# Two sums of squares of a decoder kernel folded by VectorE before TensorE sums them, and the order of its start rewritten

## The chip, the cores and the metric

The kernel runs on one core of a Trainium2 chip. The metric is the device time of one execution in microseconds. Beside it one execution was profiled; all rows below are of that one.

## The reference, cut to what matters

Two layers (DEPTH = 2) over 256 tokens of 1024 features. Each layer: RMSNorm of x, one wide projection that feeds three mixers (a gated linear recurrence, a retention, a windowed attention), gates, an output projection; a cross-attention into 256 memory tokens; a product-key mixture of 16384 single-neuron experts, the largest part. A last RMSNorm. What the change touches:

```python
def rmsnorm(x, g):
    y = x * rsqrt(mean(x * x, axis=-1) + EPS)      # over the 1024 features
    return y * g
for l in range(DEPTH):
    h = rmsnorm(x, ln_mix[l])                      # sum of x's squares, once a layer here
    ... = split(h @ w_in[l])                       # first column tiles: rq, rk, rv, rg, ...
    x = x + mixers(...)
    x = x + cross(rmsnorm(x, ln_xq[l]), rmsnorm(mem, ln_xkv[l]), ...)   # mem's squares: the same for both layers
    x = x + peer_ffn(rmsnorm(x, ln_ffn[l]), ...)
```

## The kernel before, in words

Activations lie transposed: 128 partitions by 8 chunks (KC) of 256 tokens. All weights come as a stream of 128x1024 float32 tiles (512 KB) through `ring`, four slots; a group is four tiles, and tile g.s is slot s of group g. Each tile is split into `w_hi` (rounded, by ScalarE, `high_part`, L1003) and `w_lo` (ring minus w_hi, by GpSimd, `low_part`, L445, or in some places by VectorE, `low_whole`, L1543). TensorE multiplies hi by hi, hi by lo and lo by hi (`product3`, L514 to L516); a tile of 24 products takes it 2.88 us. A slot goes round: SyncE reloads the ring slot when the low part has been made, ScalarE may write the high part when TensorE has used the slot, the low part follows, then TensorE. Each engine's program is one list in a fixed order, with waits on semaphores; an engine that waits holds up all that stands behind.

The head of a layer. Tiles 0.0 and 0.1 are multiplied by x times the gain, without the norm (`first_chunks`), then 0.2, then the sum of squares, then 0.3, then group 1 (1.0 to 1.3) with results scaled by `rinv` afterwards, then group 2 with the normed x. ScalarE squares x in four pairs of chunks (L1020); VectorE folds them to two chunks (`fold_pair`, L1575); TensorE sums those over the partitions by two products with a matrix of ones (`folded_pairs`, L485, into bank 0). ScalarE takes the root (`take_root`, L1048) after it has cast tile 0.3 and loaded the table for Sqrt; VectorE inverts it (L1585) and scales the results (`first_evac`, L1638), which frees the banks for group 1; it also makes the low part of 0.3 just ahead of the inversion (L1543). Behind the root stand ScalarE's casts of 1.0 and 1.1, whose low parts are GpSimd's first two tiles of the layer. Between folds and low part VectorE has two copies of 4 columns (L1613, L1614), in the first layer also one of 128 columns (L1581).

The start of the program. SyncE loads half tiles of 0.0 and 0.1 (front), a small table, three constants, then 0.2 and 0.3; ScalarE issues the loads of `lbp` and of x in four pieces. Both engines split the halves as they come. TensorE runs 14 products of zeros first.

The memory's squares (first layer alone). ScalarE squares the 8 chunks of mem after group HQ (L1179); after group HI TensorE sums them by eight products with ones (`rms_sums`, L477, into bank 6), ScalarE takes the root (`minv`, L1198), and the window attention goes on in the same bank. Its results' next copies out are `evac` (L1089).

## Time and profile before

| | us |
|---|---|
| runs | 2377.94, 2378.47, 2379.53 (median 2378.47) |
| the profiled execution | 2379.11 |
| its span on the core | 2377.3 |
| TensorE busy | 2360.4 (99%) |
| VectorE, ScalarE, GpSimd busy | 1595.9 (67%), 1318.1 (55%), 1068.4 (45%) |
| share of TensorE in the chain that ended last | 98% |

The chain is followed back from the last instruction; TensorE's granted clock reads 1.00 in each stretch. In rows of the timelines the first number is the start, the second the duration, both in us; brackets hold the idle time before and what ended it.

### The profile page before, as it was taken

What the parts mean: (1) busy time and instruction counts of PE and PEld (TensorE: products, weight loads), DVE (VectorE), ACT (ScalarE), POOL (GpSimd) and SP (SyncE); (2) the same over time, 40 slices, a digit from 0 to 9 for tenths busy, and PEclk for the clock granted to TensorE, in tenths of its full rate; (3) what the DMA queues carried; (4) which work ended last, traced back from release to release, by engine and by line L of the source; (5) the groups of instructions that cost most, each with busy time, mean ns of one, the idle gap of its engine ahead of it and who ended that gap; (6) DMA issues with size and microseconds to landing.
All of it is one profiled execution on the core that took longest, in us unless ns stands there. A gap on an engine that the chain in (4) does not pass through costs nothing.

```text
span 2377.3 us, 44376 instructions
## 1 busy us (share of the span) xinstructions
PE 2360.4 (99%) x16162; PEld 2152.6 (91%) x16162; DVE 1595.9 (67%) x3266; ACT 1318.1 (55%) x2054; POOL 1068.4 (45%) x445
## 2 busy tenths in 40 slices
PE   8999999999999999999999999999999999999999
PEld 7999889999999888888889998899999998888887
DVE  7465624879995656777674656168799945667776
ACT  5676555565555555554465665555555555555544
POOL 5757877787773000000067578777877720000000
PEclk9999999999999999999999999999999999999999
DMA  7544554456677667777664445545566776677774
GB/s 246 170 150 150 179 176 161 160 179 220 242 242 260 203 210 224 247 246 237 213 210 158 162 158 187 171 157 166 180 230 239 245 243 204 219 231 233 243 247 168
DMA packets 186851, 485.36 MB, mean 204 GB/s; under 512 B 14304, under 2 KB 81120, under 8 KB 182112
## 3 DMA queue, kind: packets, MB, share of 16 engines
q1 hardware_dynamic: 179376, 442.20, 56.5%
q10 hardware_dynamic: 7344, 41.36, 5.0%
q8 instruction: 88, 1.44, 0.2%
q14 instruction: 43, 0.35, 0.1%
HBM read 448.91 MB, written 34.60 MB: 203 GB/s over the span
## 4 chain that ended last, share of the span: by engine, by line
PE 98%; DVE 1%; ACT 0%; DMA 0%; POOL 0%; issue 0%; ACTq 0%; DVEq 0%
PE banks L949 29%; PE banks L514 15%; PE banks L516 15%; PE banks L515 15%; PE banks L891 5%; PE banks L550 5%; PE banks L925 3%; PE banks L892 3%; PE banks L551 2%; PE banks L854 1%; PE banks L838 1%; PE banks L819 1%; PE banks L744 0%; DMA x<-in_x 0%; PE banks L477 0%; DVE o_r L1919 0%
## 5 line engine op out<-in xcount | busy, mean ns | idle before, releaser
L445 POOL TENSOR_TENSOR w_lo<-ring,w_hi 128x1024 fp32r<-128x1024 f32 x441 | 1068.2, 2434 | 853.5 <-ACT w_hi L1003 850.5
L1003 ACT ACTIVATE w_hi<-ring 128x1024 fp32r<-128x1024 f32 x774 | 816.7, 1056 | 416.2 <-PE banks L949 339.3
L514 PE MATMUL banks<-h_r,w_hi 128*128 128x256 f32 x2464 | 701.4, 285 | 0.5 <-DVE h_r L1611 0.4
L516 PE MATMUL banks<-h_r,w_lo 128*128 128x256 f32 x2464 | 696.6, 283 | 0.0
L515 PE MATMUL banks<-h_r,w_hi 128*128 128x256 f32 x2464 | 696.4, 283 | 0.0
L949 PE MATMUL banks<-w_hi,o_r 128*128 128x512 f32 x2048 | 560.5, 390 | 0.0
L514 PEld LDWEIGHTS banks<-h_r,w_hi 128*128 128x128 f32 x2464 | 471.4, 191 | 3.4 <-issue 1.6
L515 PEld LDWEIGHTS banks<-h_r,w_hi 128*128 128x128 f32 x2464 | 471.6, 191 | 0.6 <-issue 0.5
L516 PEld LDWEIGHTS banks<-h_r,w_lo 128*128 128x128 f32 x2464 | 471.6, 191 | 0.0
L949 PEld LDWEIGHTS banks<-w_hi,o_r 128*128 128x128 f32 x2048 | 380.0, 188 | 79.3
L2093 DVE TENSOR_TENSOR w_lo<-ring,w_hi 128x1024 fp32r<-128x1024 f32 x320 | 389.6, 1218 | 31.4 <-ACT w_hi L1003 31.4
L949 PE MATMUL banks<-w_lo,o_r 128*128 128x512 f32 x1024 | 317.4, 391 | 0.0
L949 PEld LDWEIGHTS banks<-w_lo,o_r 128*128 128x128 f32 x1024 | 192.2, 188 | 42.1
L2074 DVE SCALAR_TENSOR_TENSOR arena_r<-iota_f,arena,banks 128x256 fp32r<-128x256 f32 x512 | 211.0, 473 | 0.0
L1357 ACT ACTIVATE arena<-banks 128x256 f32<-128x256 f32 (+1 forms) x192 | 73.9, 385 | 247.2 <-PE banks L516 247.0
L2125 DVE TENSOR_TENSOR o_r<-arena,o_r 128x256 fp32r<-128x256 f32 x256 | 108.4, 423 | 139.0 <-ACT o_r L1411 139.0
L891 PE MATMUL banks<-h_r,w_hi 128*128 128x512 f32 x512 | 182.8, 397 | 0.0
L892 PE MATMUL banks<-h_r,w_lo 128*128 128x256 f32 x512 | 143.6, 280 | 0.0
L1089 ACT ACTIVATE arena<-banks 128x256 f32<-128x256 f32 x116 | 44.5, 384 | 159.0 <-PE banks L516 158.9
L2119 DVE TENSOR_TENSOR arena<-arena,o_f 128x256 f32<-128x256 f32 x256 | 107.9, 421 | 18.0 <-DMA o_f<-gates_dram 4.2
L2139 DVE TENSOR_TENSOR banks<-banks,arena 128x256 f32<-128x256 f32 x64 | 27.7, 432 | 135.3 <-PE banks L949 135.3
L891 PEld LDWEIGHTS banks<-h_r,w_hi 128*128 128x128 f32 x512 | 96.2, 188 | 22.9
(332 smaller groups left out, 3123.4 us busy)
## 6 DMA issues: line engine op xcount, KB each, us to landing
ring<-in_stream SPq DMA_DIRECT2D x774, 512.0 KB, 3.4
gates_dram<-o_f ACTq DMA_DIRECT2D x32, 1024.0 KB, 5.5
o_f<-gates_dram SPq DMA_DIRECT2D x32, 1024.0 KB, 7.0
arena<-in_mem ACTq DMA_DIRECT2D x2, 1024.0 KB, 8.3
arena<-in_keys ACTq DMA_DIRECT2D x2, 1024.0 KB, 6.5
arena<-in_c_decay ACTq DMA_DIRECT2D x2, 768.0 KB, 4.8
ring<-in_stream SPq DMA_DIRECT2D x4, 256.0 KB, 6.0
x<-in_x ACTq DMA_DIRECT2D x4, 256.0 KB, 7.6
```

The lines of the kernel that those rows point to most:

```text
L445: pool.tensor_tensor(w_lo[:, s, :], ring[:, s, :], w_hi[:, s, :], ALU.subtract).then_inc(sem(f"low{s}"), 1)
L514: pe.matmul(out, lhs[0], rhs[0], start=first, stop=False)
L515: pe.matmul(out, lhs[0], rhs[1], start=False, stop=False)
L516: return pe.matmul(out, lhs[1], rhs[0], start=False, stop=last)
L550: pe.matmul(wide_out(s), hi, src[:, :, k, :], start=(k == 0), stop=False)
L891: pe.matmul(wide_out(parity), hi, h_r[:, :, k, :], start=(k == 0), stop=False)
L892: m = pe.matmul(tile_out(parity), lo, hr[0][:, k, :], start=False, stop=(k == KC - 1))
L949: m = pe.matmul(bank[:, 2 * t + half, :], gated_r[v][:, parity, t * P:(t + 1) * P], (w_hi, w_lo)[u][:, s, half * 512:(half + 1) * 512], st ...
L1003: act.activation(w_hi[:, s, :], ring[:, s, :], ACT.Copy).then_inc(sem(f"high{s}"), 1)
L2074: ins = dve.scalar_tensor_tensor(one2[:, parity, t], bc(iota_f[:, :], 1, 2), col2[:, at], bank[:, bass.ds(i, 1), :].rearrange("p a (u v t) ...
L2093: dve.tensor_tensor(w_lo[:, s, :], ring[:, s, :], w_hi[:, s, :], ALU.subtract).then_inc(sem(f"low{s}"), 1)
L2125: dve.tensor_tensor(gated_r[1][:, parity, :], product, gated_r[0][:, parity, :], ALU.subtract).then_inc(sem("gated"), 1)
```

## The change

The mem squares are made after group SQ and folded by VectorE to one chunk in three steps (`mem_folded`), so that one product with ones sums them. x's squares are folded once more (`fold_last`), with one product where two were, in both layers. ScalarE casts 1.0 and 1.1 ahead of the table load and the root, in both layers. All loads of the start are issued by SyncE, in another order; ScalarE loads the table of Exp at once; the second halves of the split of tile 0.1 come after both pieces of x; 11 products of zeros instead of 14.

```diff
@@ -366,13 +366,24 @@
 
-            for half in range(2):
-                for s in range(2):
-                    sp.dma_start(ring[:, s, half * 512:(half + 1) * 512],
-                                 a["stream"][s:s + 1, :, half * 512:(half + 1) * 512].rearrange("a p n -> (a p) n")
-                                 ).then_inc(sem(f"slot{s}_loaded" if half else f"front{s}_loaded"), 16)
-                    if s + half == 0:
-                        sp.dma_start(smalls[:, :, :], a["small"]).then_inc(sem("small_loaded"), 16)
-            for dst, src in ((freq[:, :], a["c_freq"]), (ident[:, :], a["c_ident"]), (iota_f[:, :], a["c_iota"])):
-                sp.dma_start(dst, src).then_inc(sem("consts"), 16)
+            def front(s, half):
+                cols = slice(half * 512, half * 512 + 512)
+                sp.dma_start(ring[:, s, cols], a["stream"][s:s + 1, :, cols].rearrange("a p n -> (a p) n")
+                             ).then_inc(sem(f"slot{s}_loaded" if half else f"front{s}_loaded"), 16)
+
+            def load_x(k):
+                sp.dma_start(x[:, k:k + 2, :], a["x"][:, k:k + 2, :]).then_inc(sem(f"x{k}_loaded"), 16)
+
+            sp.dma_start(lbp, a["lb"]).then_inc(sem("lb_loaded"), 16)
+            front(0, 0)
+            load_x(0)
+            sp.dma_start(smalls[:, :, :], a["small"]).then_inc(sem("small_loaded"), 16)
+            load_x(2)
+            front(1, 0)
+            front(0, 1)
+            load_x(4)
+            load_x(6)
+            front(1, 1)
             load(0, 2)
             load(0, 3)
+            for dst, src in ((freq[:, :], a["c_freq"]), (ident[:, :], a["c_ident"]), (iota_f[:, :], a["c_iota"])):
+                sp.dma_start(dst, src).then_inc(sem("consts"), 16)
 
@@ -465,3 +476,3 @@
 
-            for n in range(14):
+            for n in range(11):
                 pe.matmul(bank[:, 1, :], zeros[:, :], bc(zeros[:, :], 1, 4), start=True, stop=True)
@@ -482,6 +493,4 @@
 
-                pe.wait_ge(sem("folded"), (l + 1) * (KC // 2 - 1))
-                for k in range(2):
-                    m = pe.matmul(bank[:, 0, 0:T], ones[:, :], square[:, k, :], start=(k == 0), stop=(k == 1))
-                m.then_inc(sem("summed"), 1)
+                pe.wait_ge(sem("folded"), (l + 1) * (KC // 2))
+                pe.matmul(bank[:, 0, 0:T], ones[:, :], square[:, 0, :], start=True, stop=True).then_inc(sem("summed"), 1)
 
@@ -708,3 +717,3 @@
                 if l == 0:
-                    rms_sums(square, KC, sem("mem_squared"), 1, bank[:, 6, 0:T]).then_inc(sem("mem_summed"), 1)
+                    rms_sums(square, 1, sem("mem_folded"), 3, bank[:, 6, 0:T]).then_inc(sem("mem_summed"), 1)
                 feature_tile(G_HG, 0, T_HG, hr)
@@ -1012,5 +1021,4 @@
 
-            act.dma_start(lbp, a["lb"]).then_inc(sem("lb_loaded"), 16)
-            for k in range(0, KC, 2):
-                act.dma_start(x[:, k:k + 2, :], a["x"][:, k:k + 2, :]).then_inc(sem(f"x{k}_loaded"), 16)
+            act.wait_ge(sem("setup_dve"), 1)
+            act.activation(spare[:, :], eps[:, :], ACT.Exp)
             act.wait_ge(sem("lb_shifted"), 1)
@@ -1039,4 +1047,3 @@
                     unscaled_high(b, smalls[:, 0, 0:KC])
-                    if c == 0:
-                        half_high(1, half)
+                half_high(1, half)
             high_part(0, 2)
@@ -1074,2 +1081,4 @@
                 split_next(-1, 3)
+                split_next(G_RQ, 0)
+                split_next(G_RQ, 1)
                 act.activation(spare[:, :], eps[:, :], ACT.Sqrt)
@@ -1077,3 +1086,4 @@
                 for t in range(2 * SLOTS):
-                    split_next(G_RQ + t // SLOTS, t % SLOTS)
+                    if t > 1:
+                        split_next(G_RQ + t // SLOTS, t % SLOTS)
                     if t < SLOTS:
@@ -1141,2 +1151,5 @@
                 evac_group(G_SQ, by_feature(wqk))
+                if l == 0:
+                    act.wait_ge(sem("mem_loaded"), 16)
+                    act.activation(square, mem, ACT.Square).then_inc(sem("mem_squared"), 1)
                 evac(G_SKV, 0, sv_cols.rearrange("p (a t) -> p a t", a=1))
@@ -1176,5 +1189,2 @@
 
-                if l == 0:
-                    act.wait_ge(sem("mem_loaded"), 16)
-                    act.activation(square, mem, ACT.Square).then_inc(sem("mem_squared"), 1)
                 parts(rrms, branch_r[0][:, 0, :, :], "ret_out", 1, 1, "branch_high")
@@ -1565,4 +1575,3 @@
                         unscaled_low(k, smalls[:, 0, 0:KC], 0)
-                    if c == 0:
-                        half_low(1, half)
+                half_low(1, half)
 
@@ -1572,3 +1581,3 @@
                 if b > 1:
-                    dve.wait_ge(sem("folded"), l * (KC // 2 - 1) + b - 1)
+                    dve.wait_ge(sem("folded"), l * (KC // 2) + b - 1)
                 o = square[:, 0:2, :]
@@ -1576,2 +1585,7 @@
 
+            def fold_last(l):
+
+                dve.wait_ge(sem("folded"), l * (KC // 2) + KC // 2 - 1)
+                dve.tensor_tensor(square[:, 0, :], square[:, 0, :], square[:, 1, :], ALU.add).then_inc(sem("folded"), 1)
+
             low_whole(0, 2)
@@ -1579,2 +1593,3 @@
                 fold_pair(0, b)
+            fold_last(0)
             dve.wait_ge(sem("consts"), N_CONST)
@@ -1710,2 +1725,8 @@
                 dve.tensor_tensor(st, bank[:, 0:4, 0:3 * P], decay, ALU.mult).then_inc(sem("ret_decayed"), 1)
+                if l == 0:
+                    dve.wait_ge(sem("mem_squared"), 1)
+                    for n in (4, 2, 1):
+                        dve.tensor_tensor(square[:, 0:n, :], square[:, 0:n, :], square[:, n:2 * n, :], ALU.add
+                                          ).then_inc(sem("mem_folded"), 1)
+                        dve.wait_ge(sem("mem_folded"), {4: 1, 2: 2, 1: 3}[n])
                 out_of_banks(T_HF)
@@ -2221,2 +2242,3 @@
                         fold_pair(l + 1, b)
+                    fold_last(l + 1)
```

## Rows read from the trace of the kernel before

**Rows 1.** TensorE's waits, whole span: us in total, times, longest.

```profile
PE banks L514 <- POOL w_lo L445: 4.1, 4, 1.1
PE banks L586 <- ACT o_r L1025: 3.7, 3, 1.9
```

**Rows 2.** The chain in order of time, the memory's sum: start us, us, what.

```profile
121.71 3.46 PE banks L477 x16
```

**Rows 3.** VectorE timeline, window stage of both layers: start us, us, what.

```profile
110.60 1.76 DVE L1731 SCALAR_TENSOR_TENSOR arena<-banks,arena 128x1536 f32<-128x1536 f32 x1 [1.88 <-PE banks L682]
...
164.12 0.69 DVE L1827 COPY banks<-arena 128x512 f32<-128x512 f32 x1 [10.09 <-ACT arena L1169]
...
1294.07 1.76 DVE L1731 SCALAR_TENSOR_TENSOR arena<-banks,arena 128x1536 f32<-128x1536 f32 x1 [1.88 <-PE banks L682]
...
1344.15 0.69 DVE L1827 COPY banks<-arena 128x512 f32<-128x512 f32 x1 [10.10 <-ACT arena L1169]
```

**Rows 4.** ScalarE timeline, first layer, the memory's squares and root.

```profile
110.31 1.91 ACT L1179 ACTIVATE arena<-arena 128x2048 f32<-128x2048 f32 x1
...
130.37 1.28 ACT L1198 ACT_TABLE_LOAD   x1
131.66 0.47 ACT L1198 ACTIVATE minv<-banks,eps 128x256 f32<-128x256 f32 x1
...
133.37 0.38 ACT L1089 ACTIVATE arena<-banks 128x256 f32<-128x256 f32 x1
```

**Rows 5.** GpSimd timeline, head of the second layer.

```profile
1204.52 2.38 POOL L445 TENSOR_TENSOR w_lo<-ring,w_hi 128x1024 fp32r<-128x1024 f32 x1 [11.13 <-ACT w_hi L1003]
1208.65 11.87 POOL L445 TENSOR_TENSOR w_lo<-ring,w_hi 128x1024 fp32r<-128x1024 f32 x5 [1.75 <-ACT w_hi L1003]
```

**Rows 6.** VectorE timeline, head of the second layer.

```profile
1197.57 2.27 DVE L1575 TENSOR_TENSOR arena<-arena 128x512 f32<-128x512 f32 x3
1199.75 0.16 DVE L1613 COPY low<-lower_all 128x4 f32<-128x4 f32 x1
...
1200.15 1.22 DVE L1543 TENSOR_TENSOR w_lo<-ring,w_hi 128x1024 fp32r<-128x1024 f32 x1
1203.53 1.75 DVE L1585 RECIPROCAL rinv<-rinv 128x256 f32<-128x256 f32 x1 [2.16 <-ACT rinv L1048]
```

**Rows 7.** ScalarE timeline, head of the second layer.

```profile
1197.95 1.04 ACT L1003 ACTIVATE w_hi<-ring 128x1024 fp32r<-128x1024 f32 x1
```

**Rows 8.** TensorE timeline, the second layer's first product of tile 0.3.

```profile
1202.64 0.47 PE L514 MATMUL banks<-o_r,w_hi 128*128 128x256 f32 x1
```

**Rows 9.** VectorE timeline, beside GpSimd in the first two.

```profile
114.87 3.32 DVE L1611 TENSOR_TENSOR o_r<-arena,o_r 128x1024 fp32r<-128x1024 f32 x1
...
500.68 2.45 DVE L2040 TENSOR_SCALAR arena<-arena 128x128 uint32<-128x128 uint32 x1
...
1650.07 0.21 DVE L2040 TENSOR_SCALAR arena<-arena 128x128 uint32<-128x128 uint32 x1
```

**Rows 10.** GpSimd timeline, the same two stretches.

```profile
114.72 2.39 POOL L445 TENSOR_TENSOR w_lo<-ring,w_hi 128x1024 fp32r<-128x1024 f32 x1 [1.39 <-ACT w_hi L1003]
...
495.88 7.16 POOL L445 TENSOR_TENSOR w_lo<-ring,w_hi 128x1024 fp32r<-128x1024 f32 x3 [1.76 <-ACT w_hi L1003]
```

**Rows 11.** ScalarE timeline, head of the first layer.

```profile
13.00 1.06 ACT L1003 ACTIVATE w_hi<-ring 128x1024 fp32r<-128x1024 f32 x1
...
13.97 2.18 ACT L1020 ACTIVATE arena<-x 128x512 f32<-128x512 f32 x4
```

**Rows 12.** VectorE timeline, head of the first layer.

```profile
18.09 1.23 DVE L1543 TENSOR_TENSOR w_lo<-ring,w_hi 128x1024 fp32r<-128x1024 f32 x1
```

**Rows 13.** DMA issues from 12.5 to 13.5 us: KB each, us to landing.

```profile
ring<-in_stream SPq DMA_DIRECT2D x1, 512.0 KB, 5.8
```

**Rows 14.** TensorE timeline, start of the program.

```profile
1.18 4.87 PE L467 MATMUL banks<-zeros 128*128 128x512 bf16 x14 [1.18 <-DVE ones L1516]
7.90 0.47 PE L586 MATMUL banks<-o_r,w_hi 128*128 128x256 f32 x2 [1.85 <-ACT o_r L1025]
```

More of the change, by code:

```diff
@@ L365, in load @@
                              ).then_inc(sem(f"slot{s}_loaded"), 16)
-            for half in range(2):
-                for s in range(2):
-                    sp.dma_start(ring[:, s, half * 512:(half + 1) * 512],
-                                 a["stream"][s:s + 1, :, half * 512:(half + 1) * 512].rearrange("a p n -> (a p) n")
-                                 ).then_inc(sem(f"slot{s}_loaded" if half else f"front{s}_loaded"), 16)
-                    if s + half == 0:
-                        sp.dma_start(smalls[:, :, :], a["small"]).then_inc(sem("small_loaded"), 16)
+            def front(s, half):
[14 more added lines that the diff above has]
+            front(1, 1)
+            load(0, 2)
+            load(0, 3)
             for dst, src in ((freq[:, :], a["c_freq"]), (ident[:, :], a["c_ident"]), (iota_f[:, :], a["c_iota"])):
                 sp.dma_start(dst, src).then_inc(sem("consts"), 16)
-            load(0, 2)
-            load(0, 3)
             def refill(g, s):
```

## The prediction

> **What bounds the kernel now.** TensorE is busy for 99% of the span and makes 98% of the chain that ended last, so I read its waits first, then what stands around each place that the change touches. In the whole span it waits four times for GpSimd's low parts, 4.1 us, and three times in the unnormed products, 3.7 us [rows 1]. The first four are at the heads of the two layers, two in each: GpSimd's first low part of the second layer starts at 1204.52, its second at 1208.65 after an idle gap [rows 5], because ScalarE's casts of tiles 1.0 and 1.1 stand behind the root. The other place is the memory's sum, 3.46 us of TensorE's own work on the chain [rows 2]. A change outside TensorE's path is worth nothing here; one on it counts in full. I make the sum against the span of 2377.3 us; the profiled execution's 2379.11 lies 0.6 above the median of 2378.47, so a difference is carried over to the median as it is.
>
> **The memory's sum.** Eight products become one: 3.46 / 8 = 0.43 us stays, 3.03 goes. That it comes through is seen from the second layer, which makes no such sum: from the first window softmax to the copy behind the second one it needs 1344.15 - 1294.07 = 50.08 us, the first layer 164.12 - 110.60 = 53.52 [rows 3]. The difference, 3.44, is the whole sum. What the first layer keeps is the root: a table load of 1.28 and 0.47 of work, ahead of the copy at 133.37 [rows 4], and VectorE's inversion of the same numbers. With TensorE 3.03 earlier these are later in relation to it. Following the queues, I find the copies that free its two banks late by 0.2 to 0.3 us at three places, 0.6 together; the bounds are 0 (the second layer shows no loss) and 1.75 (root and table load in full). **Term: -3.03 + 0.6 = -2.4, between -3.0 and -1.3.** ScalarE's squares (1.91, [rows 4]) move to group SQ, where each tile of 2.88 us leaves ScalarE idle for 1.55; they make one copy 0.3 late, and GpSimd is three tiles ahead. VectorE's three folds (128x1024, 512, 256: about 1.2, 0.7, 0.4 us, by the 1.22 of a 128x1024 subtraction in [rows 6] and the 0.76 of one 128x512 fold there) fall in its idle 17 us before the window's rotation. Queued behind them is that rotation, about 5 us ahead of its use. Both cost nothing; were that cover gone, it would be 2 to 4 us.
>
> **x's second fold, and the head of the second layer.** One product of 0.43 goes on TensorE. VectorE gets a fold of 128x256, 0.4 us. The larger edit is the order on ScalarE. It ends the cast of 0.3 at 1199.0 [rows 7]; the slots of 0.0 and 0.1 are then free and 1.0, 1.1 have long landed, so their casts end at 1200.1 and 1201.1, the table load at 1202.4, and the root starts at about 1202.7, 0.3 earlier than before. GpSimd can start at 1200.1 instead of 1204.52 [rows 5].
>
> Taken alone, that is a gain: both waits (2.1) and the 0.43 go, 0.6 comes back before 1.2, whose cast still stands behind the normed chunks, and the next bound is VectorE's scaling chain. Result -1.85.
>
> But VectorE is not done. Its three folds run from 1197.57 for 2.27, to 1199.84; with the fourth it is 1200.3. Then come two small copies and the low part of 0.3, before at 1199.75, 1199.95 and 1200.15 [rows 6], all from local memory to local memory, all now while GpSimd works. What that does the trace shows in two places. A VectorE subtraction of 128x1024 with both inputs local took 3.32 us beside a GpSimd subtraction that had begun 0.15 before it; the same kind takes 1.22 otherwise [rows 6, 9, 10]: it waited for the whole 2.39 of the other. And when GpSimd has three in a row (from 495.88 for 7.16), a small VectorE operation of 0.21 took 2.45 [rows 9, 10]: the one just ahead of it had got in, and GpSimd then took its next tile first. So VectorE gets one such operation in for each GpSimd tile. The Trainium skill, page "SBUF — State Buffer", section "Who interferes with whom", says that VectorE and GpSimd share a pair of ports as an exclusive lock, taken by copies and scalar operations that use both ports and by operations with two local inputs. By that rule the order of ScalarE's casts would be paid for on VectorE; the trace agrees with 3.32 and 2.45 against 1.22 and 0.21. Without the rule the two heads below would sum to -3.1, with it to +3.2.
>
> Here GpSimd has two tiles ready: 1.0 to about 1202.7, 1.1 (cast by 1201.1) to about 1205.2. One of the small copies waits for the first, the other for the second, and the low part of 0.3 is made from about 1205.4 to 1206.7, where it was ready at 1201.37. TensorE began 0.3 at 1202.64 [rows 8], a little slowed, as if at 1202.8; it now begins at 1206.7, +3.9. Against that both waits for GpSimd are gone, -2.1: **+1.8**. The inversion, right behind the low part, starts at 1206.7 instead of 1203.53 [rows 6], +3.2; less the 1.06 for which VectorE waited for TensorE in its scaling chain, group 2's banks come free 2.1 later, but they had 0.4 to spare: again +1.7. **Term: +1.7, between -1.85 (no such blocking) and +3.2 (the inversion's delay in full).** If only the low part is blocked, by one tile of 2.4, it is ready at 1203.9, TensorE starts 1.1 later there and ends 1.15 earlier.
>
> **The head of the first layer.** Two edits. The start: TensorE's first real product is at 7.90 after an idle 1.85 [rows 14], with 3.7 us of such waits in all [rows 1], of which 0.5 is in the second layer. With x in the same queue as the weights, in the order of use, and both engines splitting in that order, I expect its unnormed products to end some 2 us earlier; the cast of 0.2, at 13.00 before [rows 11], by about 1 to 1.7. Three products of zeros fewer end no later than the first real one begins, since 14 take 4.87 us [rows 14] and TensorE waits after them; bounds 0 and, if its clock were not up, some 2 us. Then the same race. Let E be the end of the cast of 0.2 (14.06 before). VectorE began the low part of 0.3 at 18.09 [rows 12], E + 4.0; with the fourth fold E + 4.45. ScalarE does four squares in 2.18 [rows 11] and the casts of 0.3 and 1.0, so GpSimd can start at E + 4.15, if tile 1.0 has landed. It is 0.3 us ahead, in front of the last small copy and the low part, and tile 1.1 follows. With E about 12.7, the low part of 0.3 is ready near 22.8 where it was 19.3, TensorE is 3.5 later, less its two waits of 2.0: **+1.5, between -1.8 (no blocking, start in full) and +2.2**. If tile 1.0 lands a little later than I think, VectorE goes first and this is about -1.4.
>
> Also new: the root now stands behind the landing of 1.1. A tile asked for at 13.1 took 5.8 us to land [rows 13]; asked for at about 12.2 it lands by 18.0, the root comes at 20.5 at the latest, which the blocked inversion hides.
>
> **The sum.** -2.4 + 1.7 + 1.5 = +0.8: 2378.1 of span, and 2378.47 + 0.8 = **2379.3**.
>
> **The rivals.**
> 1. The race goes as above in the second layer, but in the first VectorE is ahead, or only one tile blocks: -2.4 + 1.7 - 1.4 = -2.1, or -2.4 - 1.15 - 1.1 = -4.65. 2373.8 to 2376.4. For it: 0.3 us decide. Against: in the second layer nothing depends on a landing.
> 2. No blocking that matters (operations of 4 columns don't take the ports, or GpSimd yields): -2.4 - 1.85 - 1.25 = -5.5, **2373.0**. For it: no row shows so small an operation beside GpSimd; against it rows 9, and that the low part itself is one of the kind that waited.
> 3. Slower: the root behind the landing of 1.1. If it lands at 24 or later in the first layer, the root comes at 26.5, 7 us late, and scaling and group 1 with it: +7 less the waits saved gives +5.5 there, in sum +4.8 or more, **2383.3**. It decides from a landing 12 us after the issue; the longest near it took 5.8 [rows 13].
> 4. The change does nothing on TensorE: the memory's gain is eaten by the copies behind the root (1.75) and the heads are even: -1.3, 2377.2. This lies inside the first case's spread.
>
> **How the numbers follow.** About 0.2%, 4.8 us, is what a measurement of this kernel can tell from no change. Chances: the forecast 0.50; rival 1 0.22; rival 2 0.15; rival 3 0.05; rival 4 0.08. Rival 2 and the lower end of rival 1 are faster by over 0.2%, in all 0.17; slower is rival 3 and a little of the forecast's upper end (both terms at their bounds, +3.2 + 2.2 - 1.3 = +4.1), 0.06; within, 0.77. The forecast's own range is 2377 to 2381.5. The range reaches down to rival 2: 2373.5 to 2381.5.
>
> **What would show it.** In the profile after: L477 one product of 0.43, TensorE's waits for L445 gone at the heads; instead waits for VectorE's L1543; the small copies at the heads lasting up to 2.4 us; the low part of 0.3 in the second layer ready about 5 us after the folds; the inversion later than before. Wrong if those copies still take 0.2 beside a busy GpSimd (then rival 2), or if the stretch between the softmaxes of the first layer shrinks by less than 2 us.

## The result and the profile after

The changed kernel took 2383.82 us (median of 16 runs, 2382.49 to 2385.12), the kernel before, run beside it, 2378.69 (16 runs, 2377.94 to 2380.31). The ratio is 1.0021, 95% interval 1.0014 to 1.0028: 5.1 us slower, where the forecast said 0.8 slower with a range up to 2381.5. The profiled execution took 2383.58, its span is 2381.8, that of before 2377.3.

TensorE's waits, over the whole span (total, times, longest), are the first view:

```profile
PE banks L523 <- issue: 8.9, 2, 5.2
...
PE banks L523 <- DVE w_lo L1553: 0.5, 1, 0.5
...
PE banks L523 <- ACT arena L1099: 0.4, 1, 0.4
```

The four waits for GpSimd's low parts of [rows 1] are gone, as forecast, and so are most of the waits in the first products. In their place stand two stretches of 5.2 and 3.7 us ahead of the product of tile 0.3, which the view can't name ("issue"). VectorE's timeline at the head of the second layer names it (start, duration):

```profile
1198.69 2.27 DVE L1584 TENSOR_TENSOR arena<-arena 128x512 f32<-128x512 f32 x3
1201.00 0.43 DVE L1589 TENSOR_TENSOR arena<-arena 128x256 f32<-128x256 f32 x1
1201.34 2.39 DVE L1628 COPY low<-lower_all 128x4 f32<-128x4 f32 x1
1203.77 2.26 DVE L1629 TENSOR_SCALAR oml<-low 128x4 f32<-128x4 f32 x1
1206.06 1.23 DVE L1553 TENSOR_TENSOR w_lo<-ring,w_hi 128x1024 fp32r<-128x1024 f32 x1
1207.20 1.75 DVE L1600 RECIPROCAL rinv<-rinv 128x256 f32<-128x256 f32 x1
```

And GpSimd's there:

```profile
1201.32 4.68 POOL L456 TENSOR_TENSOR w_lo<-ring,w_hi 128x1024 fp32r<-128x1024 f32 x2 [6.80 <-ACT w_hi L1012]
```

GpSimd began its two tiles at 1201.32, 0.02 ahead of the first small copy. The copies of 4 columns, each of which took less than 0.2 in the kernel before [rows 6], took 2.39 and 2.26, and the low part of 0.3 was ready at 1207.3, 5.9 after the last fold. The head of the first layer is the same picture: GpSimd at 17.85, the copies at 17.88 for 2.35 and at 20.26 for 2.26, the low part at 22.56.

What the forecast did not have is in the windows (busy time of TensorE with its instructions, its weight loads, VectorE, ScalarE, GpSimd, then TensorE's granted clock, the DMA share, GB/s):

```profile
22.00:24.00 2.00, 0.12 (x1) 0.15 (x1) 1.97 (x3) 0.00 (x0) 0.50 (x1) 0.87 0.00 0
24.00:26.00 2.00, 2.00 (x10) 2.00 (x11) 1.97 (x3) 0.00 (x0) 0.00 (x0) 0.50 0.57 135
26.00:28.00 2.00, 2.00 (x15) 2.00 (x15) 1.96 (x6) 0.60 (x1) 0.00 (x0) 0.78 0.86 305
28.00:30.00 2.00, 2.00 (x19) 2.00 (x18) 2.00 (x6) 1.54 (x2) 0.08 (x1) 1.00 0.83 315
...
1205.00:1207.00 2.00, 0.00 (x0) 0.00 (x0) 1.97 (x2) 0.00 (x0) 1.00 (x1) 1.00 0.00 0
1207.00:1209.00 2.00, 1.61 (x9) 1.64 (x10) 1.97 (x3) 0.00 (x0) 0.00 (x0) 0.73 0.30 53
1209.00:1211.00 2.00, 2.00 (x12) 2.00 (x11) 1.97 (x6) 0.31 (x1) 0.00 (x0) 0.50 0.94 352
```

TensorE stood idle until 23.89, and its granted clock was at 0.50, the 1.2 GHz level, from 23.5 to about 27; in the second layer it came back at 1207.39, and the clock was at 0.50 from 1207.9 to 1211.2. In that time it began a product every 0.215 us instead of every 0.12 (the windows count 10 from 24 to 26, and 19 once the clock is at 1.00, with those that reach in from the window before).

The memory's part shows between the same two marks as in [rows 3]:

```profile
113.88 1.76 DVE L1752 SCALAR_TENSOR_TENSOR arena<-banks,arena 128x1536 f32<-128x1536 f32 x1 [1.88 <-PE banks L691]
...
165.29 0.69 DVE L1848 COPY banks<-arena 128x512 f32<-128x512 f32 x1 [9.71 <-ACT arena L1182]
```

165.29 - 113.88 = 51.41, where it was 53.52: 2.11 shorter.

To see where the time goes I compare five marks, all on VectorE or the end: A, its multiplication at L1706 behind the head (63.42 before); B, the copy at L1827 (164.12); C, the first fold for the second layer (1197.57); D, L1706 in the second layer (1246.89); and the span. The differences from the first profile of before, as steps from mark to mark, for all kernels of this study (the last step carries the rounding of the span, 0.05):

| kernel (profile) | to A: first head | A to B: memory | B to C | C to D: second head | D to end | span |
|---|---|---|---|---|---|---|
| changed | +3.28 | -2.11 | -0.05 | +2.36 | +1.02 | +4.5 |
| changed, e8 | +3.59 | -2.11 | -0.06 | +1.29 | +1.09 | +3.8 |
| changed, e15 | +2.40 | -2.11 | -0.02 | +2.36 | +0.97 | +3.6 |
| changed, e16 | +3.56 | -2.11 | +1.26 | +3.57 | +1.02 | +7.3 |
| before, e13 | -0.89 | 0.00 | +0.02 | -0.03 | +1.00 | +0.1 |
| before, e14 | -0.77 | 0.00 | -1.02 | +0.27 | +1.02 | -0.5 |
| e1 casts behind | -0.64 | -2.10 | -1.04 | -0.45 | +0.03 | -4.2 |
| e2 cast order only | +0.34 | 0.00 | -0.01 | -1.16 | +0.64 | -0.2 |
| e3 zeros in the gap | +1.88 | -2.11 | -1.07 | +1.22 | -0.01 | -0.1 |
| e4 GpSimd held | -0.86 | -2.10 | -0.58 | -1.66 | 0.00 | -5.2 |
| e5 three folds | +0.40 | -2.09 | -1.03 | -1.25 | +0.97 | -3.0 |
| e6 cast order and fold | +3.72 | 0.00 | -0.05 | +2.19 | +1.03 | +6.9 |
| e7 copies early, held | +1.21 | -2.10 | -0.07 | -1.64 | +0.01 | -2.6 |
| e9 memory only | -0.91 | -2.10 | -0.70 | +0.02 | -0.01 | -3.7 |
| e10 start only | -0.68 | 0.00 | -1.01 | +0.74 | +1.07 | +0.1 |
| e11 root between | -1.00 | -2.12 | -0.78 | -0.49 | +0.99 | -3.4 |
| e12 order by layer | -0.82 | -2.10 | -0.44 | -1.64 | +1.01 | -4.0 |

### The profile page after: what moved, and what is told of

The parts are those of the page before. It is cut to its first block, busy times and chain, and to the rows that moved or that the text cites. A ratio compares the mean times of both kernels' runs of the same rounds, so it can differ in the third digit from the quotient of the medians.

```text
span 2381.8 us, 44341 instructions
## 1 busy us (share of the span) xinstructions
PE 2360.6 (99%) x16141; PEld 2152.2 (90%) x16141; DVE 1610.6 (68%) x3271; ACT 1319.1 (55%) x2055; POOL 1069.7 (45%) x445
## 4 chain that ended last, share of the span: by engine, by line
PE 96%; ACT 1%; DVE 1%; issue 1%; DMA 0%; SPq 0%; DVEq 0%
PE banks L958 29%; PE banks L523 15%; PE banks L525 15%; PE banks L524 15%; PE banks L900 5%; PE banks L559 4%; PE banks L934 3%; PE banks L901 3%; PE banks L560 2%; PE banks L863 1%; PE banks L847 1%; PE banks L828 1%; DVE o_r L1940 1%; PE banks L753 0%; ACT w_hi L1012 0%
```

## The experiments

Runs sent together share a chip and the runs of the kernel before; each time below stands beside the median of before in its own call.

### e1 to e4: which edit, what kind of loss, and a cure

**e1**, the changed kernel with ScalarE's order at the heads undone. (In e1, e10, e11 and e12 the result of ScalarE's early table load, one element, also goes to a column of its own instead of `spare`; the excerpts here don't show it.)

```diff
                 split_next(-1, 3)
-                split_next(G_RQ, 0)
-                split_next(G_RQ, 1)
                 act.activation(spare[:, :], eps[:, :], ACT.Sqrt)
                 take_root(l * 3, 0)
                 for t in range(2 * SLOTS):
-                    if t > 1:
-                        split_next(G_RQ + t // SLOTS, t % SLOTS)
+                    split_next(G_RQ + t // SLOTS, t % SLOTS)
```

> The changed kernel with one edit undone: ScalarE casts tiles 1.0 and 1.1 behind the root again. Theory A (this order alone makes the loss, since GpSimd then works while VectorE makes its small copies and the low part of 0.3): TensorE's two idle stretches of 5.2 and 3.7 us and the stretches at a granted clock of 0.50 behind them are gone, the waits for GpSimd's low part are back (about 2.1 in the second layer), and the memory's gain of 2.15 and the gain at the start stay: 2374.5, between 2373.5 and 2376. Rival B (the loss sits in the start or in the memory's squares): no better than 2381.

Measured: 2375.42 (before 2378.12; ratio 0.9990, 0.9981 to 0.9999). The waits for GpSimd are back (3.3 us in three), the small copies last 0.17 again, and the largest "issue" wait left is 0.9. Without this order the change is a gain.

**e2**, the kernel before with that order as its only edit (the lines above, the other way round).

> The kernel before with ScalarE's order at the heads as its only edit (1.0 and 1.1 cast ahead of the root). Theory A: both heads lose as in the changed kernel: +2.5 in the second layer, and in the first +3.5, as it has no gain at the start to set against it; 2384.5 (2383 to 2386), with idle stretches of over 3 us ahead of the product of 0.3 and a granted clock of 0.50 behind each. Rival B (the order costs nothing by itself): 2377 to 2379.

Measured: 2377.47 (before 2378.12; 0.9998, 0.9989 to 1.0007). No idle stretch ahead of 0.3 and no loss in time. Two things cancel in it: the second head is 1.16 shorter, and the first, +0.34, is 0.9 behind the mean of the three profiles of before (e13 and e14 below), as ScalarE waited 1.37 us for tile 1.1 to land before it could take the root. So theory A, and with it the forecast's "the order of ScalarE's casts would be paid for on VectorE", does not hold as it stands. VectorE's rows and GpSimd's in the first layer say why:

```profile
16.70 0.22 DVE L1584 CAST iota<-iota_f 128x128 bf16<-128x128 f32 x1
16.95 0.17 DVE L1616 COPY low<-lower_all 128x4 f32<-128x4 f32 x1
17.15 0.17 DVE L1617 TENSOR_SCALAR oml<-low 128x4 f32<-128x4 f32 x1
17.36 1.23 DVE L1546 TENSOR_TENSOR w_lo<-ring,w_hi 128x1024 fp32r<-128x1024 f32 x1
```

```profile
17.39 5.80 POOL L445 TENSOR_TENSOR w_lo<-ring,w_hi 128x1024 fp32r<-128x1024 f32 x2 [16.94 <-ACT w_hi L1003]
```

VectorE reached its low part at 17.36, GpSimd its tile at 17.39: VectorE was 0.03 ahead, and here it is GpSimd that waits (5.80 for two tiles that take 4.7 otherwise). In the changed kernel a fold of 0.43 stands ahead of these rows on VectorE.

**e3**, the changed kernel with products of zeros where TensorE would stand idle:

```diff
                 folded_pairs(l)
+                for n in range(15 if l else 22):
+                    pe.matmul(bank[:, 3, :], zeros[:, :], bc(zeros[:, :], 1, 4), start=True, stop=True)
                 pe.wait_ge(sem("consts"), N_CONST)
```

> The changed kernel, but TensorE makes products of zeros (22 in the first layer, 15 in the second, into a bank that nobody reads before it is overwritten) between the sum and the first product of 0.3, as long as it would have stood idle. Theory A (the idle time itself is the one cost and the fall of the clock behind it a second one, 14 products at 0.215 instead of 0.12 us in the first layer and some 16 in the second): the granted clock stays at 1.00 and 2.9 us come back, 2380.9 (2380.3 to 2381.5). Rival B (the clock falls for another reason than the idle time, or costs nothing): 2383.8. If the zeros run beyond the idle time, up to 0.5 more in each layer.

Measured: 2379.42 (before 2378.12; 1.0007, 0.9998 to 1.0016). The blocking of VectorE is there unchanged (copies of 2.37 and 2.26 in the first layer), and in that layer the product of 0.3 begins 6.6 us behind the start of the fourth fold, as in the changed kernel (23.18 - 16.56, 23.89 - 17.28); yet 3.8 us are back (5.1 slower becomes 1.3). The clock stays at 1.00:

```profile
17.79 4.91 PE L621 MATMUL banks<-zeros 128*128 128x512 bf16 x22
```

```profile
22.00:24.00 2.00, 1.52 (x11) 0.95 (x9) 2.00 (x2) 0.00 (x0) 0.00 (x0) 1.00 0.02 4
24.00:26.00 2.00, 2.00 (x19) 2.00 (x18) 1.93 (x5) 0.00 (x0) 0.00 (x0) 1.00 0.81 258
26.00:28.00 2.00, 2.00 (x19) 2.00 (x18) 2.00 (x7) 1.00 (x2) 0.00 (x0) 1.00 0.60 225
```

The first head is 1.88 late instead of 3.21 (mean of the four profiles of the changed kernel), the second 1.22 instead of 2.40: the clock behind the idle stretch costs 1.3 and 1.2, about as expected from the products at half clock. (In the second layer the product of 0.3 comes 0.14 sooner behind the fourth fold than in the changed kernel, so some 0.1 of the 1.2 is not the clock's.) The time lies below the expected range, 2380.3 to 2381.5; in the profiled execution the two other stretches were some 1.0 shorter each, which is told of under e13 to e16.

**e4**, the changed kernel with one wait on GpSimd (`low3` is what VectorE's low part of 0.3 signals):

```diff
                 if l:
                     low_part(l * GROUPS, 2)
+                pool.wait_ge(sem("low3"), l * GROUPS + 1)
```

> The changed kernel, but GpSimd waits with its tile 1.0 in each layer until VectorE has made the low part of 0.3. Theory A (two tiles of GpSimd block VectorE there, and nothing else is wrong with the order): the small copies last 0.2 again, the low part of 0.3 is ready near 1202.6 in the second layer, TensorE doesn't idle, GpSimd still has 1.0 and 1.1 in time, and neither the idle time nor the waits for GpSimd remain: 2372.5 (2371.5 to 2374). Rival B (with GpSimd 1.3 us later, TensorE waits for tile 1.0 or 1.1 as in the kernel before, or the inversion is blocked and the scaled chunks come late): 2375 to 2377.

Measured: 2374.55 (before 2378.12; 0.9985, 0.9976 to 0.9994), 3.6 faster and between the two expected ranges. The small copies last 0.17, GpSimd begins at 1198.53, right behind the low part, and is in time with both tiles; the 0.7 us for which TensorE still waits for its low parts are for tile 1.2, once in each layer. Second head -1.66. The first gives only -0.86, which is hardly better than the kernel before itself in e13 and e14.

### e5 to e8: the two edits together

**e5**, the changed kernel with x's fourth fold undone (`fold_last` and its calls out, two products again, the counts of `folded` as before).

> The changed kernel with x's fourth fold undone: three folds and two products, everything else as changed. The run with the cast order alone lost nothing: in it VectorE began the low part of 0.3 at 17.36 and GpSimd its tile 1.0 at 17.39, where in the changed kernel VectorE came to its small copies at 17.88 and GpSimd was at work from 17.85. Theory C (the loss is made by two edits together: the fourth fold of 0.43 makes VectorE lose a race that ScalarE's order has made close): without the fold VectorE is ahead by 0.3 to 0.4 us, the low part of 0.3 is not blocked in either layer, no idle stretch, no fall of the clock: first head -0.8, memory -2.1, second head -1.2 against the kernel before, 2374.0 (2373 to 2375.5). Theory A (ScalarE's order makes the loss by itself once the start is changed too): both idle stretches stay, 2382 or more. Between them, 2377 to 2379, if the race is lost in one layer.

Measured: 2375.75 (before 2379.18; 0.9986, 0.9977 to 0.9995). VectorE's low part begins at 17.29, GpSimd at 17.31; 1197.44 and 1197.48 in the second layer. VectorE is ahead by 0.02 and 0.04, less than expected, but ahead; nothing on VectorE is blocked, and the gains of the memory's part and of the second head are there. The first head is +0.40, much as in e2 (+0.34): TensorE there waits 2.3 us for the scaled copies: ScalarE waited 1.50 for tile 1.1 to land before it could take the root.

**e6**, the kernel before with both edits, the order and the fold, and nothing else.

> The kernel before with ScalarE's order and x's fourth fold together, nothing else. Each of them alone costs nothing that was seen. Theory C (the two together lose the race): idle stretches ahead of the product of 0.3 and a granted clock of 0.50 behind them, as in the changed kernel: +3.6 to +4.4 in the first head, +2.4 in the second, and 2378.1 + 6.4 = 2384.5 (2383 to 2386). Rival (the changed start is needed for it in the first layer): +2.4 alone, 2380.5. If the race is decided by less than 0.1 us, one head may go either way: 2378 to 2381.

Measured: 2386.30 (7 runs; before 2379.18; 1.0028, 1.0017 to 1.0039). The waits of the changed kernel exactly:

```profile
PE banks L512 <- issue: 8.9, 2, 5.2
```

```profile
17.39 4.65 POOL L445 TENSOR_TENSOR w_lo<-ring,w_hi 128x1024 fp32r<-128x1024 f32 x2 [16.93 <-ACT w_hi L1001]
```

```profile
17.16 0.22 DVE L1588 CAST iota<-iota_f 128x128 bf16<-128x128 f32 x1
17.42 2.35 DVE L1620 COPY low<-lower_all 128x4 f32<-128x4 f32 x1
19.80 2.26 DVE L1621 TENSOR_SCALAR oml<-low 128x4 f32<-128x4 f32 x1
22.09 1.22 DVE L1544 TENSOR_TENSOR w_lo<-ring,w_hi 128x1024 fp32r<-128x1024 f32 x1
```

GpSimd starts at 17.39 as in e2; VectorE arrives at 17.42, behind it by 0.03 instead of ahead by 0.03. The order alone makes no such stretch (e2), nor does a fourth fold without the order (e1, where the other edits stand beside it); the two together put the heads at +3.72 and +2.19. This settles theory C.

The 0.03 us are not chance. Both queues hang on the cast of tile 0.2 in the first layer: GpSimd's tile begins 5.12 us behind the start of that cast; VectorE gets to its first small copy 5.15 behind it with a fourth fold, and to the low part of 0.3, past the copies, 5.09 behind it without. That is so within 0.01 in all four profiles of the changed kernel and in e2, e5 and e6, though the cast itself begins anywhere from 11.83 to 12.90.

**e7**, e4 with VectorE's small copies moved away from the folds: the two of 4 columns to the end of the layer before, the cast of the iota behind the inversion.

> The changed kernel, GpSimd's first tile 1.0 held back until the low part of 0.3 is made, and VectorE's small copies (the layer's bounds, the cast of the iota) moved out of the stretch between the folds and that low part. Theory: the low part of 0.3 comes 0.4 to 0.65 earlier than with the hold alone, GpSimd starts as much earlier, and TensorE's two waits for its low part (0.7 in all) shrink to nothing or to 0.2: 0.3 to 0.7 below the run with the hold alone, 2374.1 (2373.5 to 2374.7). Rival (TensorE is bound by VectorE's scaling chain behind the root there): the same as the run with the hold alone, 2374.5, with its waits for the scaled copies, 1.3, grown by what the others shrank.

Measured: 2376.79 (before 2379.18; 0.9990, 0.9981 to 0.9999), 2.4 faster where 4 was expected: a miss, and both halves teach something. In the second head it is -1.64 against -1.66 with the hold alone: GpSimd began 0.42 sooner, and nothing came of it. TensorE's last two waits there, 0.4 us for the low part of tile 1.2 and 0.3 for a scaled copy, lie 14.25 and 20.55 us behind the first fold in both kernels; the cast of 1.2 stands behind the normed chunks, and those behind the root, which kept their times. The rival holds. In the first the iota's cast, now beside GpSimd's second tile and ahead of the first scaled copy, took 1.02 instead of 0.22; TensorE stood idle for 2.5 us, came back at 0.72 and 0.50, and the head is 2.1 later than with the hold alone.

**e8**, the changed kernel again, beside the others.

> The changed kernel once more, on the chip of the others and beside them. In its first profile both layers ran a stretch of wide products (four tile groups from 260 and from 1460 us) at 2.83 us for one copy to the next, where the kernel before had 2.83 in the first layer and 2.77 in the second, and three of the four kernels tried so far 2.77 in both: 1.1 us of the span for each layer. Theory P (the pace is drawn anew in each execution): it may show 2.77 here in either layer, and its span is then 1.1 or 2.2 lower, with both idle stretches and both stretches at 0.50 as before. Rival Q (the pace belongs to the kernel): 2.83 in both again. The time: 2383.3 (2382.5 to 2384.2) either way, 0.5 lower than in its first runs if this chip is the one on which the kernel before took 2378.1.

Measured: 2384.66 (9 runs; before 2379.18; 1.0024, 1.0014 to 1.0034), 5.5 slower and above the expected range. Both idle stretches (5.2, 3.7) are there, and both stretches of wide products are at 2.83 (rival Q). In this execution the clock stayed at 1.00 behind the second idle stretch, and that head lost 1.29 instead of 2.36: about what e3 gives for the clock. In e16 it stayed at 0.50 for some 6 us behind the second and the head lost 3.57, so the price goes from 0 to 2.3 in single executions.

### e9 to e12: the parts alone, and better versions

**e9**, the kernel before with the memory's part alone (squares moved, three folds, one product).

> The kernel before with the memory's part alone: the squares made in group SQ, folded by VectorE, one product. From the first layer's first softmax to the copy behind the second one the changed kernel and three of its variants were 2.09 to 2.11 us shorter than the kernel before. Theory: the same 2.1 here, all of it in that stretch, and the span shorter by that: 2.1 below the kernel before. Rival (part of it is given back by a copy behind the late root, and the other edits hid that): 1.3 or less.

Measured: 2377.09 (before 2379.07; 0.9990, 0.9981 to 0.9999), 2.0 faster. The stretch is 2.10 shorter.

**e10**, the kernel before with the start alone (loads, table, halves, 11 products of zeros).

> The kernel before with the start alone changed: SyncE loads x between the weights, the halves split in that order, 11 products of zeros, ScalarE's table loaded early; the order behind it (root ahead of the casts of 1.0 and 1.1) and three folds as before. Theory: TensorE's waits in its first products fall from 3.2 us to 1.3 or 2, but the cast of 0.2 still waits for its landing near 12 to 12.7 (13.00 before), and everything behind it is 0.3 to 0.7 earlier: the mark behind the first head 0.3 to 0.6 earlier, and the time 0.3 to 0.6 below the kernel before, which is not to be told from no change. Rival (the forecast's term: unnormed products done 2 us earlier, 1 to 1.7 kept): 1.0 or more below it.

Measured: 2378.89 (before 2379.07; 0.9995, 0.9986 to 1.0004): no gain that can be told. TensorE's waits in the first products fell from 3.2 us to 1.6, but the cast of 0.2 began at 12.21, having waited for its landing, and from 8 to 12 us:

```profile
6.00:8.00 2.00, 1.00 (x6) 0.83 (x6) 1.09 (x5) 1.11 (x3) 0.00 (x0) 1.00 0.77 251
8.00:10.00 2.00, 1.69 (x9) 1.72 (x10) 1.82 (x4) 1.82 (x4) 0.00 (x0) 0.68 1.06 400
10.00:12.00 2.00, 2.00 (x12) 2.00 (x11) 2.00 (x6) 1.84 (x5) 0.00 (x0) 0.50 1.02 414
```

The clock fell to 0.50 here too (also in e2 and e12 near the same place), so that products that started earlier ran slower; but that does not decide it: e12 and e1 have the same first layer, the clock fell in e12 and not in e1, and their heads are -0.82 and -0.64. The DMA engines were full (1.06, 1.02). In the three profiles of before and the four of the changed kernel the cast of 0.2 begins 0.02 us behind its tile's landing, and the load is issued at 4.89 to 5.80 before and at 5.46 or 5.47 after: the new order did not bring that tile sooner.

**e11**, e4 with ScalarE's order between the two: 1.0, root, 1.1.

> The changed kernel, GpSimd's tile 1.0 held back until the low part of 0.3 is made, and ScalarE's order in the middle between the two: it casts 1.0, then takes the root, then casts 1.1. Theory: 1.0 is in time for GpSimd, the root no longer waits for the landing of 1.1 (for which ScalarE waited 0.35 to 1.5 us in the first layer of the kernels that cast it first) and comes 1 us earlier in both layers; the waits for the scaled copies (1.3 to 3.0) become 0.5 or less. First head -1.5, memory -2.1, second head -1.9 against the kernel before: 5.0 to 5.5 below it. Rival (1.1 comes late instead, or the inversion is now blocked by GpSimd, as the earlier root puts it beside tile 1.0): no better than the run with the hold alone, 3.6 below the kernel before.

Measured: 2377.05 (before 2379.07; 0.9990, 0.9981 to 0.9999). A miss: the root is early (inversion at 18.84), but 1.1's cast came only at 22.83, behind the first normed chunk, its low part at 23.96, and TensorE waited 1.6 for it, and 2.1 in the second layer. The rival holds, by another queue than I had thought of.

**e12**, e4 with the first layer's ScalarE order and GpSimd as before, and the second layer's as in e4:

```diff
                 if l:
                     low_part(l * GROUPS, 2)
+                    pool.wait_ge(sem("low3"), l * GROUPS + 1)
...
-                split_next(G_RQ, 0)
-                split_next(G_RQ, 1)
+                for t in range(2 * l):
+                    split_next(G_RQ, t)
```

> The changed kernel with its first layer's ScalarE order as before (root, then the casts) and its second layer's as changed with GpSimd held back. Theory (the marks add up): first head -0.64 as with the casts behind, memory -2.1, second head -1.66 as with the hold: 4.4 below the kernel before in the profile, apart from the pace of the wide products, which is worth 1.1 for each layer and falls either way. Rival: the heads are not independent (the ring's slots run on), and the sum is off by over 1.

Measured: 2374.58 (before 2379.07; 0.9979, 0.9970 to 0.9988): 4.5 us below the kernel before, the best of the study by its ratio, though e4's interval overlaps it. The marks add up as said.

### e13 to e16: what is drawn anew in each execution

Both kernels, unchanged, were profiled twice more.

> The kernel before, profiled once more. Theory P (the pace of the wide products and the landing of tile 0.2 are drawn anew in each execution): the copies in each layer are 2.77 or 2.83 us apart as it falls; the cast of 0.2 begins between 11.5 and 13.0 and the mark behind the first head moves with it, up to 0.9 earlier than in the first profile; span 2375 to 2377.5. Theory Q (both belong to the kernel): 2.83 in the first layer and 2.77 in the second, the cast at 13.0, span 2377.3 within 0.3.

> The kernel before a third time. As for the second: by theory P at least one of the two layers, or the cast of 0.2, differs from the first or the second profile; by theory Q all three are as in the first.

> The changed kernel a third time. By theory P its copies may now be 2.77 us apart in a layer, and its span 1.1 or 2.2 below 2381.8; by theory Q they are 2.83 apart in both layers, as in its first two profiles. Both idle stretches (5.2 and 3.7) are there again; the granted clock falls to 0.50 behind the first, and behind the second it may (first profile) or may not (second profile), which is worth 1.1.

> The changed kernel a fourth time, as for the third: 2.83 in both layers again would be six of six for theory Q within this kernel, one 2.77 decides for theory P. Idle stretches as before; the fall of the clock behind the second one in some of the four profiles only.

Measured: 2379.58 and 2378.91 for the kernel before, 2382.82 and 2386.39 for the changed one (one run each; before in that call 2378.89). The stretch in question is one of wide products (L550 before), where VectorE's additions out of the banks (L1930, L1951 after the change; the expectations call them copies) follow each other. VectorE's rows at the same place in the second layer, the first profile of before and then of after:

```profile
1484.27 0.42 DVE L1930 TENSOR_TENSOR arena<-banks,arena 128x256 f32<-128x256 f32 x1 [1.89 <-ACT arena L1096]
1487.04 0.42 DVE L1930 TENSOR_TENSOR arena<-banks,arena 128x256 f32<-128x256 f32 x1 [2.35 <-ACT arena L1096]
```

```profile
1488.25 0.42 DVE L1951 TENSOR_TENSOR arena<-banks,arena 128x256 f32<-128x256 f32 x1 [2.04 <-ACT arena L1106]
1491.08 0.42 DVE L1951 TENSOR_TENSOR arena<-banks,arena 128x256 f32<-128x256 f32 x1 [2.41 <-ACT arena L1106]
```

2.77 against 2.83 us, all else equal and the granted clock at 1.00 in both; over a layer it makes 1.0 to 1.1 us. For the kernel before it is drawn: 2.83 and 2.77 in the two layers, then 2.83 twice, then 2.77 and 2.83. For the changed kernel it was 2.83 in eight layers of eight. Theory P holds for the one, Q so far for the other. Over all profiles: every layer in whose head TensorE stood idle for 2.5 us or more behind its first products had the slow pace (11 of 11: the changed kernel, e6, and e7's first layer); of the 25 others 9 had it. Against a tie: in e14 TensorE stood idle for 2.5 us ahead of its first real product, and that layer was at 2.77. e3, where TensorE is kept busy and all else is as changed, had 2.77 in both. What ties the pace to the gap is not shown, and with one profile of most kernels it may still be partly chance. A second thing that varies lies between B and C, near 750 us, where VectorE waits for the first `gates_dram` load: it waited 3.8 us in e1, 4.8 in e12 and 5.5 in e16, and TensorE stood still for it for 0, 0.3 and 1.0. From e1 to e12 the distance grows by 0.6 there and nowhere else, so that "B to C" is not the pace alone.

The first head of the kernel before varies as well: 0, -0.89, -0.77, with the cast of 0.2 at 13.00, 12.16 and 12.05. Against the mean of the three the changed kernel's heads are +3.76 and +2.32, and the stretches with the pace +0.97; with the memory's -2.11 that is +4.9, beside 5.1 between the medians.

## Why the prediction was wrong

**What bounds the kernel:** right. Every difference that could be placed lies on TensorE's path.

**The memory's sum, -2.4:** measured -2.1: -2.09 to -2.12 in twelve profiles of nine kernels. Where 0.6 was forecast to come back through late copies, 0.92 did. Set beside the timeline of before, TensorE falls behind at two products: by 0.69 at 135.79, which waited for `evac` (0.42 in the view, but it begins 0.70 behind the one ahead of it where 0.12 is usual, and the next one is slow too), and by 0.24 at 153.59, for which the view names no wait. The squares and folds cost nothing, though the folds took 7.02 us in all where the forecast had 2.3 (1.73, 2.75 and 2.47): they have two local inputs, and a GpSimd tile was under way as each began. Their cover was large enough, and the first head and the stretch up to the softmax were late by the same 3.28.

**The head of the second layer, +1.7:** the mechanism came as described: GpSimd at work by the time the fourth fold ends, one small copy behind each of its tiles, the low part last, both old waits gone. The Trainium skill's rule that the forecast used (page "SBUF — State Buffer", section "Who interferes with whom": an exclusive lock, held for the whole instruction by whoever comes first) agrees with the 2.39 and 2.26. With the clock kept up the step is +1.2 (e3), +1.3 (e8). The step of the forecast that failed is the price of the idle time: it took TensorE's delay less its saved waits, and had no term for slower products behind an idle stretch. The 3.3 us at a granted clock of 0.50 behind it add 1.1 to 1.2 on average, and the step measured +2.3.

**The head of the first layer, +1.5:** here the forecast fell furthest, +3.8 against the mean of before. Two things. The clock again, 1.3. And the start: of the "2 us earlier", "1 to 1.7" kept, nothing remained. The cast of 0.2 began at 12.73, 12.20, 11.83 and 12.90 in four profiles of the changed kernel, 12.4 on average, and at 13.00, 12.16 and 12.05 before, also 12.4; each time 0.02 behind its landing, with the DMA engines full (a share of 1.02 to 1.04 from 8 to 12 us in the changed kernel). To read the 3.2 us of waits ahead of it in one profile (3.7 less 0.5, [rows 1]; 1.85 of them in [rows 14]) as something that this tile would gain was the error.

**In the sum**, forecast and marks differ by 4.1 us (+0.8 and +4.9): 2.5 for the clock, 1.4 for the start (the end of the cast of 0.2 at 14.06 in [rows 11] and at 12.7 in the forecast), 0.3 for the memory, 1.0 for the stretches with the pace, of which the forecast knew nothing and whose cause is open, less the rest, some 1.0, by which the heads' other terms were too dear (the second, 1.1 without the clock where 1.7 was forecast; the first, 2.5 without the clock where 2.9 was forecast without the start's gain). Of the 1.0, 0.25 is one wait of 1.0 in e16 alone, spread over four profiles.

**Which rule of the forecast the runs corrected:** it put the blocking down to ScalarE's order. e1, e2, e5 and e6 show that order and fold are needed both. The race was named for the first layer ("0.3 us decide"); it is closer than that, 0.02 to 0.04 us either way, and stands in both layers. In the first layer GpSimd came ahead of the first small copy, not of the last one: the two small copies waited for its two tiles, and the low part came behind both, unblocked.

**The rivals.** No blocking (2373.0) and one tile (2373.8 to 2376.4) did not come, but they are what e5, e4 and e12 look like. Rival 3's mechanism, the root behind the landing of 1.1, is real: ScalarE waited 0.35 to 1.50 us for it in the first layer; in the changed kernel the blocked inversion hid that, as the forecast said, and in e5 it did not. Its place as the one way to be slower was the mistake: none of the cases gave the idle time more than its own length, so that none but this one reached past 2381.5.

## What to carry to other kernels

Price an idle stretch of TensorE twice, once for its length and once for the products behind it at half clock; in a gap that can't be removed, products of zeros buy the second part back. When two engines share a lock, write down when each arrives, and count a margin of a few hundredths of a us as no margin: it held from execution to execution, as both queues hang on the same cast, but an edit of 0.4 us on one of them turned it, and 2.3 us for each tile hung on it. One wait that fixes the order is cheap (e4). And before a start-up is credited with a gain, look at what the DMA engines are doing and at more than one profile of the kernel before: the first real mark moved by 0.9 us without any edit.

## What the runs showed of the hardware

- TensorE came back to a granted clock of 0.50, or fell to it within 0.6 us, after 5.2 us of idle time (five profiles of five, the changed kernel and e6), after 3.7 us in four of five (it stayed 1.00 in e8) and after 2.5 us in e7, but not after 2.5 us in the start of e14, 2.3 in e5 or 2.1 in e11. It also fell near 8 to 10 us, in the start of e2, e10 and e12, where TensorE had been busy for 1.0 of the 2 us from 6 to 8; e1, e5 and e7 were no busier there (1.0 to 1.1), the kernel before far less (0.15), and it did not fall. What decides is not shown. It went back to 1.00 after 3 to 6 us of work. The Trainium skill, page "TensorE: Matmul & The Clock Gate", section "HAM oscillation — how this bites in real kernels", describes such a loss behind waits for data; the runs agree with it but for e8's second stretch, and a head lost 1.1 to 1.3 us to it on average, from nothing (e8) to 2.3 (e16).
- Who came first at the lock was decided by 0.02 to 0.04 us, and the same way each time: GpSimd ahead by 0.02 or 0.03 in all eight heads of the changed kernel's four profiles and both of e6, VectorE ahead by 0.02 to 0.04 in the four of e2 and e5. In e3's second head GpSimd was ahead by 0.01 and the first small copy still took 0.16; the second took 2.25 and the low part 3.33.
- The same stretch of products at a granted clock of 1.00 ran at one of two paces, 2.77 or 2.83 us for a tile, and held it mostly for the whole stretch; in e4 and e11 the first tile of the first layer was at 2.83 and the rest at 2.77.
